# Down matrices of the experts loaded as one 16 KB run per partition, with a step of four in the gate/up products

## The chip, the cores and the metric

One core of a Trainium2 chip runs the whole program. The metric is the time of one execution on the device in microseconds, as the median of several runs. The profile comes from one further execution, taken by the hardware profiler.

## What is computed

A trunk of two layers over 512 tokens of 1024 channels, all in float32. Layer 0 mixes the tokens by latent attention with 16 heads, layer 1 by a bidirectional gated linear recurrence. Behind each mixer stands a mixture of 32 experts, of which each token uses two of one group of four:

```
idx, wts = route(ht, w_router, router_bias)        # two experts for each token
g, u = split(xb @ w_gu[e], 2)                      # w_gu[e]: 1024 x 1024, 512 gate and 512 up columns
y = (silu(g) * u) @ w_dn[e]                        # w_dn[e]: 512 x 1024
x = x + g2 * sum over the two experts of wts * y
```

Each expert has 4 MB of gate/up weights and 2 MB of down weights, and every expert of both layers is read once: 64 x 6 MB, about 400 MB.

## The kernel before

Before the experts of a layer run, its mixer, the norm, the router and a ranking of the tokens have run (the stages of `STAGES`). The change touches none of it.

**Blocks.** The expert work is cut into 60 blocks of 32 token rows per layer (`NB`, `ROWS`). A table `CAP` gives the busier experts up to five blocks and the quieter ones a single block; `RUN` and `BLOCKS` fix in which order they come, experts with many blocks mixed with those that have one. Which expert stands at which place is known at run time only: SP reads it from `order_i`. A loop over `more_i` could run blocks beyond the 60, for tokens that fit in none.

**Gathers and scatters.** GpSimd gathers 32 token rows for each block from `xn_dram` (L639), four blocks to a tile, and scatters each block's result to `ys_dram` (L646).

**TensorE.** A tile of four blocks is transposed by `rows_transposed` (L1030), whose stationary operand is read with a step of 8 floats (`chunk(1, k)`). `gate_up` (L1034 to L1041) runs for each block k = 0 to 7 over the 1024 channels, and for each k four products side by side, `s_` = 0 to 3: stationary is the block's transposed rows, 128 x 32, moving are 256 columns of the gate/up matrix (128 gate and the 128 up columns that belong to them), and the results go to partitions 32 s_ to 32 s_ + 31 of a PSUM bank. So four column tiles of 32 work beside each other, and quarter s_ of the hidden units lies in 32 partitions of its own. In float32 each product is two matmul records. A half of `gate_up` (four values of k) is 16 products, 32 records. Between the halves stands the transpose of the block before (L1044), behind them its down products.

ScalarE takes the silu of the gate part (L1362), VectorE multiplies with the up part (L1937), TensorE transposes the 128 x 128 result (L1044), ScalarE copies it (L1350). `down` (L1046 to L1051) then takes f = 0 to 3: stationary is piece f of the copy, 128 hidden units x 32 rows, moving are 256 of the 1024 columns of row group f of the down matrix. As quarter s_ of the hidden units is columns 128 s_ to 128 s_ + 127, row group f must hold rows 128 f to 128 f + 127 of the down matrix, one to a partition: this is what `dn_rows` (L423) says. VectorE scales the result by the token's weight and the gate (L1919).

**Weights.** A ring of three slots, each for one gate/up and one down matrix (`GU`, `DN`), is filled by SP alone, one matrix behind the other on its queue: `load_expert` (L506 to L514) waits until the gate/up products of the expert three places before are done (L510), issues the gate/up matrix (L511), waits for the down products of that expert (L513) and issues the down matrix (L514). The gate/up matrix is taken as `(p k) n -> p (k n)`: partition p holds rows 8p to 8p + 7, one run of 32 KB. The down matrix is taken as `(k p) n -> p k n`: partition p holds rows p, 128 + p, 256 + p and 384 + p, four runs of 4 KB. The matrices of the first two places are issued earlier, while the mixer's last products and the router run (L481 to L487 and L498 to L504). TensorE waits for the matrices at L1077 and L1062, when the first block of an expert comes.

Of the kernel before, what the change touches and what calls it, by code (L numbers as in the profile page):

```python
# [12 lines left out]
P = 128  # L13
# [18 lines left out]
FT = FE // P  # L32
# [16 lines left out]
TILES = P // ROWS  # L49
# [28 lines left out]
RING = 3  # L78
# [67 lines left out]
def trunk(nc, x, c, positions, norm_mix, norm_ffn, w_ada, b_ada, mla_w_in, mla_q_a_norm, mla_kv_a_norm,  # L146
# [4 lines left out]
    with ctx:  # L151
# [70 lines left out]
        def view(t, off, *dims):  # L222
            n = 1
            for d in dims:
                n *= d
            v = t[:, off:off + n]
            if len(dims) == 2:
                v = v.rearrange("p (a b) -> p a b", a=dims[0])
            elif len(dims) == 3:
                v = v.rearrange("p (a b c) -> p a b c", a=dims[0], b=dims[1])  # L230
            assert len(dims) < 4
            return v

        hT = view(arena, 0, KT, SEQ)
        w_in = view(arena, 4096, KT, LAT)
# [95 lines left out]
        S = {}  # L331
# [70 lines left out]
        DN = [view(ring_dn0, 0, FT, D), view(ring_dn1, 0, FT, D), view(arena, 8192, FT, D)]  # L402
# [14 lines left out]
        def gone(place, l):  # L417
            return NB * l + LAST[ORDER[place]] + 1

        def gu_rows(l, e):  # L420
            return moe_w_gu[l, e].rearrange("(p k) n -> p (k n)", k=KT)

        def dn_rows(l, e):  # L423
            return moe_w_dn[l, e].rearrange("(k p) n -> p k n", p=P)


        @block.sync
        def _(sp):
# [26 lines left out]
            def load_xb(b):  # L455
                xcols = slice(D + b * 2 * P, D + (b + 1) * 2 * P)
                sp.dma_start(w_xb, rnn_w_in[0][:, xcols].rearrange("(k p) n -> p k n", p=P)).then_inc(S["wx_in"], 16)

            def load_gt(b):
                gcols = slice(b * 2 * P, (b + 1) * 2 * P)  # L460
                sp.dma_start(w_gt, rnn_w_in[0][:, gcols].rearrange("(k p) n -> p k n", p=P)).then_inc(S["wg_in"], 16)

            def load_rg(b):
                for m, w in enumerate((rnn_w_rf, rnn_w_if, rnn_w_rb, rnn_w_ib)):
                    sp.dma_start(w_rg[:, 2 * m:2 * m + 2, :], w[0, b].rearrange("(k p) n -> p k n", p=P)
                                 ).then_inc(S["wr_in"], 16)

            for l in range(2):
                if l == 0:
                    sp.wait_ge(S["sq_used"], 2 * TT)  # L470
                    sp.dma_start(w_o, mla_w_o[0].rearrange("(k p) n -> p k n", p=P)).then_inc(S["w_o_in"], 16)
                    sp.wait_ge(S["ada_used"], 12)
                    for r in range(2 * KT):
                        for j in range(3):
                            if r:
                                sp.wait_ge(S["stage_used"], 3 * (r - 1) + j + 1)
                            ch = 3 * (r // KT) + j
                            sp.dma_start(stage[:, j, :], w_ada_v[1][:, r % KT, ch * D:(ch + 1) * D]
                                         ).then_inc(S[f"stage_in{j}"], 16)
                    sp.wait_ge(S["unit"], STAGES["proj0"] + 8)  # L480
                    sp.dma_start(GU[0].rearrange("p k n -> p (k n)"), gu_rows(l, 0)).then_inc(S["gu_in0"], 16)  # L481
                    sp.dma_start(DN[0], dn_rows(l, 0)).then_inc(S["dn_in0"], 16)
                    sp.wait_ge(S["xn_ready"], 4 * 2)
                    sp.dma_start(xn_dram.rearrange("(i p) d -> p i d", p=P), xn_moe).then_inc(S["xn_saved"], 16)
                    sp.dma_start(DN[1], dn_rows(l, 1)).then_inc(S["dn_in1"], 16)
                    sp.wait_ge(S["unit"], STAGES["ada1g"] + 4)
                    sp.dma_start(GU[1].rearrange("p k n -> p (k n)"), gu_rows(l, 1)).then_inc(S["gu_in1"], 16)  # L487
                else:
                    sp.dma_start(w_o, rnn_w_o[0].rearrange("(k p) n -> p k n", p=P)).then_inc(S["w_o_in"], 16)
                    for b in range(1, NBLK):  # L490
                        sp.wait_ge(S["unit"], STAGES[f"xb{b - 1}"] + 2)
                        load_xb(b)
                        sp.wait_ge(S["unit"], STAGES[f"gate_r{b - 1}"] + 2)
                        load_gt(b)
                        sp.wait_ge(S["unit"], STAGES[f"rg{b - 1}"] + 8)
                        load_rg(b)
                    sp.wait_ge(S["y_ready"], NBLK)
                    sp.dma_start(GU[1].rearrange("p k n -> p (k n)"), gu_rows(l, 1)).then_inc(S["gu_in1"], 16)  # L498
                    sp.wait_ge(S["unit"], STAGES["proj1"] + 8)
                    sp.dma_start(GU[0].rearrange("p k n -> p (k n)"), gu_rows(l, 0)).then_inc(S["gu_in0"], 16)  # L500
                    sp.dma_start(DN[0], dn_rows(l, 0)).then_inc(S["dn_in0"], 16)
                    sp.wait_ge(S["xn_ready"], 4 * 4)
                    sp.dma_start(xn_dram.rearrange("(i p) d -> p i d", p=P), xn_moe).then_inc(S["xn_saved"], 16)
                    sp.dma_start(DN[1], dn_rows(l, 1)).then_inc(S["dn_in1"], 16)  # L504

                def load_expert(n):  # L506
                    o = ORDER[n]
                    e = sp.value_load(order_i[o:o + 1, 0:1], min_val=0, max_val=NE - 1)
                    if n >= RING:
                        sp.wait_ge(S["gu_done"], gone(n - RING, l))  # L510
                    sp.dma_start(GU[n % RING].rearrange("p k n -> p (k n)"), gu_rows(l, e)).then_inc(S[f"gu_in{n % RING}"], 16)  # L511
                    if n >= RING:
                        sp.wait_ge(S["dn_done"], gone(n - RING, l))  # L513
                    sp.dma_start(DN[n % RING], dn_rows(l, e)).then_inc(S[f"dn_in{n % RING}"], 16)  # L514

                sp.wait_ge(S["order_ready"], l + 1)
                sp.wait_ge(S["more_ready"], l + 1)
                for n in range(2, NE):
                    load_expert(n)
                if l == 0:  # L520
                    sp.wait_ge(S["gu_done"], gone(NE - RING, l))
                    sp.wait_ge(S["dn_done"], gone(NE - RING, l))
                    load_xb(0)
                    load_gt(0)
                    load_rg(0)

                o = OV[l]
                sp.wait_ge(S["more_ready"], l + 1)
                n_more = sp.value_load(more_i[0:1, 31:32], min_val=0, max_val=MAX_EXTRA)
                sp.wait_ge(S["gu_done"], NB * (l + 1))  # L530
                sp.wait_ge(S["dn_done"], NB * (l + 1))
                with sp.Fori(0, MAX_EXTRA) as u:
                    with sp.If(n_more > u):
                        e = sp.value_load(more_i[0:1, bass.ds(u, 1)], min_val=0, max_val=NE - 1)
                        sp.wait_ge(o["dn_done"], u + 1)
                        sp.dma_start(GU[0].rearrange("p k n -> p (k n)"), gu_rows(l, e)).then_inc(o["w_in"], 16)
                        sp.dma_start(DN[0], dn_rows(l, e)).then_inc(o["w_in"], 16)

                sp.wait_ge(S["ov_done"], l + 1)
                for i in range(TT):  # L540
                    sp.dma_start(y_pair[i // 2][:, i % 2, :], y_rows[i]).then_inc(S[f"y_in{i}"], 16)
# [141 lines left out]
        def _(pe):  # L683
# [223 lines left out]
            for l in range(2):  # L907
# [126 lines left out]
                def gate_up(pb, rows, w, ks):  # L1034

                    for k in ks:
                        pair = w[:, k, :].rearrange("p (two s f) -> p two s f", two=2, s=TILES)
                        for s_ in range(TILES):
                            last = mm(ps[s_ * ROWS:(s_ + 1) * ROWS, pb, 0:2 * QF].rearrange("p (a b) -> p a b", a=2),  # L1039
                                      rows[:, k, :], pair[:, :, s_, :], start=(k == 0), stop=(k == KT - 1))  # L1040
                    return last  # L1041
# [27 lines left out]
                for n in range(NB):  # L1069
                    o, j = BLOCKS[n]  # L1070
# [22 lines left out]
                o = OV[l]  # L1093
# [19 lines left out]
        def _(act):  # L1113
# [167 lines left out]
            for l in range(2):  # L1281
# [33 lines left out]
                if l == 0:  # L1315
                    columns1("ada1a", 2)
                modulated(2 * l + 1)
                (_, g), = mine(f"logits{l}", 1, "A")
                act.wait_ge(S["unit"], g + 1)
                A(scores.rearrange("p i e -> p (i e)"), bank(g)[:, 0:TT * NE], ACT.Sigmoid).then_inc(S["a_free"], 1)  # L1320
# [669 lines left out]
```

## Time and profile before

| | |
|---|---|
| median of 3 runs | 1841.3 us (1840.11 to 1847.21) |
| profiled execution | 1844.75 us |
| its span | 1843.0 us |
| TensorE busy | 1459.4 us (79%) |
| DMA | 517.14 MB, mean 281 GB/s |
| expert stage of layer 0 | about 444 to 957 us |
| expert stage of layer 1 | about 1297 to 1808 us |

A busy time counts the moments in which at least one instruction of the engine runs. The DMA share is that of 16 engines, and a packet is one contiguous piece as an engine moved it. The clock granted to TensorE is at one of two levels, 1.2 or 2.4 GHz; the column PEclk is its mean as a part of the upper one.

### The profile page before, as it was taken

How to read it: one execution, taken by the hardware profiler on the slowest of the kernel's cores; microseconds unless marked ns; L12 is line 12 of the kernel's file. 1: busy time of each engine (PE TensorE's matmuls, PEld its weight loads, DVE VectorE, ACT ScalarE, POOL GpSimd, SP SyncE). 2: the span in 40 equal slices, each digit the busy share in tenths (PEclk: the TensorE clock that was granted, in tenths of full speed). 3: DMA queues.
4: the chain of work that ended last, by engine and by line, in shares of the span. 5: the costliest groups of instructions: out<-in, count | busy, mean ns of one | idle time of the engine just before them, and what ended most of it. 6: DMA issues, size and time to landing. Idle time of an engine off the chain costs nothing.

```text
span 1843.0 us, 34668 instructions
## 1 busy us (share of the span) xinstructions
PE 1459.4 (79%) x14391; PEld 834.5 (45%) x14391; DVE 656.7 (36%) x1130; ACT 340.1 (18%) x776; POOL 309.3 (17%) x356
## 2 busy tenths in 40 slices
PE   3999999997977877987744999796887678888852
PEld 3644777475533444544322444335454334444420
DVE  5674776745110111111103399875211111111102
ACT  3344444111100100111002233211111001111100
POOL 1001111001321222222100111100331113122200
PEclk9999999976988988999876999895898889899976
DMA  9634222575899999999974221034799999999994
GB/s 370 246 140 160 80 70 90 174 294 198 340 398 410 391 402 406 387 402 403 421 299 183 65 92 48 1 131 189 268 383 396 400 406 390 395 395 408 416 417 161
DMA packets 89853, 517.14 MB, mean 281 GB/s; under 512 B 12859, under 2 KB 25556, under 8 KB 80242
## 3 DMA queue, kind: packets, MB, share of 16 engines
q1 hardware_dynamic: 76176, 497.96, 69.1%
q0 software_dynamic: 11616, 16.85, 2.9%
q8 instruction: 110, 1.80, 0.4%
q10 hardware_dynamic: 1922, 0.29, 0.1%
q14 instruction: 29, 0.24, 0.0%
HBM read 507.70 MB, written 22.02 MB: 287 GB/s over the span
## 4 chain that ended last, share of the span: by engine, by line
PE 49%; DMA 33%; DVE 11%; issue 3%; ACT 2%; SPq 1%; POOLq 1%; POOL 0%; DVEq 0%; ACTq 0%
DMA ring_gu<-in_moe_w_gu_dram 26%; PE ps L1039 15%; PE ps L1049 7%; DMA arena<-in_moe_w_gu_dram 4%; PE ps L956 3%; PE ps L732 3%; PE ps L841 3%; PE ps L868 3%; PE ps L921 2%; DMA ring_gu<-in_w_ada_dram 2%; DVE ring_dn L1735 2%; PE ps L775 2%; PE ps L854 2%; PE ps L755 2%; PE ps L803 1%
## 5 line engine op out<-in xcount | busy, mean ns | idle before, releaser
L1039 PE MATMUL ps<-ring_gu,arena 128*32 128x256 f32 x4992 | 336.2, 409 | 120.8 <-DMA ring_gu<-in_moe_w_gu_dram 116.6
L1937 DVE TENSOR_TENSOR arena<-arena,ps 128x128 f32<-128x128 f32 x120 | 34.5, 288 | 748.0 <-ACT arena L1362 748.0
L1039 PEld LDWEIGHTS ps<-ring_gu,arena 128*32 128x32 f32 x4992 | 167.5, 116 | 246.5 <-DMA ring_gu<-in_moe_w_gu_dram 86.2
L646 POOL DMA_INDIRECT ys_dram<-arena,out_idx x120 | 118.9, 991 | 773.4 <-DVE arena L1919 757.0
L1039 PE MATMUL ps<-arena 128*32 128x256 f32 x2688 | 186.2, 419 | 76.3 <-DMA arena<-in_moe_w_gu_dram 75.2
L1049 PE MATMUL ps<-ring_dn,arena 128*32 128x256 f32 x2496 | 167.9, 382 | 18.0 <-issue 15.9
L1039 PEld LDWEIGHTS ps<-arena 128*32 128x32 f32 x2688 | 91.2, 119 | 148.0 <-issue 56.7
L1350 ACT ACTIVATE arena<-ps 128x128 f32<-128x128 f32 x120 | 33.3, 278 | 644.0 <-PE ps L1044 631.8
L639 POOL DMA_INDIRECT arena<-xn_dram,tok_idx x120 | 111.4, 928 | 92.8 <-DVE out_idx L1887 56.8
L1049 PEld LDWEIGHTS ps<-ring_dn,arena 128*32 128x32 f32 x2496 | 83.8, 110 | 86.3 <-issue 35.0
L921 PE MATMUL ps<-arena 128*128 128x512 f32 x256 | 110.6, 592 | 0.9 <-ACT arena L1163 0.9
L1919 DVE SCALAR_TENSOR_TENSOR arena<-ps,wtab,gate_bc 128x256 f32<-128x256 f32 x120 | 58.1, 484 | 139.4 <-PE ps L1049 133.2
L1049 PE MATMUL ps<-arena 128*32 128x256 f32 x1344 | 90.0, 380 | 9.2 <-issue 8.4
L1362 ACT ACTIVATE arena<-ps 128x128 f32<-128x128 f32 x120 | 33.3, 278 | 257.3 <-PE ps L1039 149.1
L921 PEld LDWEIGHTS ps<-arena 128*128 128x128 f32 x256 | 48.6, 190 | 61.9 <-issue 60.7
L841 PE MATMUL ps<-ring_dn 96*128 96x512 f32 x128 | 71.1, 641 | 0.9 <-DVE ring_dn L1604 0.9
L956 PE MATMUL ps<-ring_gu,ring_dn 128*128 128x512 f32 x128 | 57.1, 609 | 12.3 <-ACT arena L1302 12.3
L1049 PEld LDWEIGHTS ps<-arena 128*32 128x32 f32 x1344 | 45.0, 110 | 46.2 <-issue 18.9
L868 PE MATMUL ps<-arena 128*128 (+1 forms) x512 | 64.3, 269 | 0.0
L868 PEld LDWEIGHTS ps<-arena 128*128 128x128 f32 x512 | 62.2, 192 | 0.1
L721 PE MATMUL ps<-ident,arena 128*128 128x128 f32 x128 | 27.8, 390 | 41.7 <-DVE arena L1460 40.8
L1250 ACT ACTIVATE arena<-ps,mla_small 128x512 f32<-128x512 f32 x64 | 44.0, 687 | 84.1 <-DVE mla_small L1621 51.9
(311 smaller groups left out, 1709.8 us busy)
## 6 DMA issues: line engine op xcount, KB each, us to landing
ring_gu<-in_moe_w_gu_dram SPq DMA_DIRECT2D x44, 4096.0 KB
ring_dn<-in_moe_w_dn_dram SPq DMA_DIRECT2D x44, 2048.0 KB
arena<-in_moe_w_gu_dram SPq DMA_DIRECT2D x20, 4096.0 KB
arena<-in_moe_w_dn_dram SPq DMA_DIRECT2D x20, 2048.0 KB
ring_gu<-in_w_ada_dram SPq DMA_DIRECT2D x12, 2048.0 KB, 20.3
ring_gu<-in_w_ada_dram SPq DMA_DIRECT2D x48, 512.0 KB, 3.6
arena<-in_rnn_w_in_dram SPq DMA_DIRECT2D x8, 1024.0 KB, 6.2
ring_dn<-ys_dram SPq DMA_DIRECT2D x8, 1024.0 KB, 8.0
```

The costliest lines, as they stand in the source:

```text
L639: g.indirect_dma_start(xg[part, t % 2, :], None, xn_dram, bass.IndirectOffsetOnAxis(ap=tok_idx[0:ROWS, col:col + 1], axis=0), bounds_check ...
L646: g.indirect_dma_start(ys_dram, bass.IndirectOffsetOnAxis(ap=out_idx[:, col:col + 1], axis=0), yo[:, n % 4, :], None, bounds_check=2 * TIL ...
L732: last = mm(bank(g), src[:, k, i * P:(i + 1) * P], w_o[:, k, hf * HALF:(hf + 1) * HALF], start=(k == 0), stop=(k == KT - 1))
L755: last = mm(bank(g)[:, 0:width], hT[:, k, i * P:(i + 1) * P], w_in[:, k, hf * HALF:hf * HALF + width], start=(k == 0), stop=(k == KT - 1))
L841: mm(ps[:, 2 + qt, :], qT[0:QK, hb, qt * P:(qt + 1) * P], kT[0:QK, hb, :], start=True, stop=True).then_inc(S["s_ready"], 1)
L868: last = mm(ps[:, 7, qv * VH:(qv + 1) * VH], probsT[:, (p - 3) % 2, kt, :], kv_tok[:, kt, at(hv), NOPE:NOPE + VH].rearrange("p o d -> p (o ...
L921: last = mm(bank(g), w[:, k, m * P:(m + 1) * P], hT[:, k, :], start=(k == 0), stop=(k == KT - 1))
L956: last = mm(bank(g), yT[:, k, i * P:(i + 1) * P], w_o[:, k, hf * HALF:(hf + 1) * HALF], start=(k == 0), stop=(k == KT - 1))
L1039: last = mm(ps[s_ * ROWS:(s_ + 1) * ROWS, pb, 0:2 * QF].rearrange("p (a b) -> p a b", a=2), rows[:, k, :], pair[:, :, s_, :], start=(k == ...
L1049: last = mm(ps[s_ * ROWS:(s_ + 1) * ROWS, pb, 0:QD], src[:, f * ROWS:(f + 1) * ROWS], w[:, f, s_ * QD:(s_ + 1) * QD], start=(f == 0), stop ...
L1250: A(probs[:, p % 2, :], ps[:, 2 + p % 4, :], ACT.Exp, bias=nmax[:, p % 4:p % 4 + 1], accum_out=rsum[:, p // 4, p % 4:p % 4 + 1]).then_inc( ...
L1919: v.scalar_tensor_tensor(out=yo[:, n % 4, :], in0=ps[:, 5 + n % 2, 0:QD], scalar=wtab[:, col:col + 1], in1=gate_bc[:, 1, l * QD:(l + 1) * ...
```

## The change

The down matrix is read as `(p k) n -> p (k n)`: partition p holds rows 4p to 4p + 3, which lie behind one another in DRAM, one run of 16 KB. Row group f of the slot is then rows f, 4 + f, 8 + f, ... So that the hidden units agree, quarter s_ of the gate/up columns becomes the columns s_, 4 + s_, 8 + s_, ...: the moving operand of `gate_up` reads with a step of four floats, in both its gate and its up part. Outputs keep their shape and place; they hold other hidden units. `down` is not changed. The first lines below are the new layout, the last the new columns; the six other issues of down matrices change in the same way as the one of `load_expert`.

```
         def dn_rows(l, e):
-            return moe_w_dn[l, e].rearrange("(k p) n -> p k n", p=P)
+            return moe_w_dn[l, e].rearrange("(p k) n -> p (k n)", k=FT)
...
-                    sp.dma_start(DN[n % RING], dn_rows(l, e)).then_inc(S[f"dn_in{n % RING}"], 16)
+                    sp.dma_start(DN[n % RING].rearrange("p k n -> p (k n)"), dn_rows(l, e)).then_inc(S[f"dn_in{n % RING}"], 16)
...
                 def gate_up(pb, rows, w, ks):
 
                     for k in ks:
-                        pair = w[:, k, :].rearrange("p (two s f) -> p two s f", two=2, s=TILES)
+                        pair = w[:, k, :].rearrange("p (two f s) -> p two s f", two=2, s=TILES)
                         for s_ in range(TILES):
                             last = mm(ps[s_ * ROWS:(s_ + 1) * ROWS, pb, 0:2 * QF].rearrange("p (a b) -> p a b", a=2),
                                       rows[:, k, :], pair[:, :, s_, :], start=(k == 0), stop=(k == KT - 1))
```

## Rows read from the trace of the kernel before

**Rows 1.** The page: busy time of the engines, DMA share in 40 slices.

```profile
PE 1459.4 (79%) x14391; PEld 834.5 (45%) x14391; DVE 656.7 (36%) x1130; ACT 340.1 (18%) x776; POOL 309.3 (17%) x356
...
DMA  9634222575899999999974221034799999999994
GB/s 370 246 140 160 80 70 90 174 294 198 340 398 410 391 402 406 387 402 403 421 299 183 65 92 48 1 131 189 268 383 396 400 406 390 395 395 408 416 417 161
```

**Rows 2.** The page: the chain that ended last, shares of the span by line.

```profile
DMA ring_gu<-in_moe_w_gu_dram 26%; PE ps L1039 15%; PE ps L1049 7%; DMA arena<-in_moe_w_gu_dram 4%; PE ps L956 3%; PE ps L732 3%; PE ps L841 3%; PE ps L868 3%; PE ps L921 2%; DMA ring_gu<-in_w_ada_dram 2%; DVE ring_dn L1735 2%; PE ps L775 2%; PE ps L854 2%; PE ps L755 2%; PE ps L803 1%
```

**Rows 3.** Windows: length, busy of PE, PEld, DVE, ACT, POOL, clock, DMA share, GB/s.

```profile
500.00:940.00 440.00, 339.74 (x5107) 185.78 (x5099) 55.09 (x152) 46.81 (x156) 91.15 (x96) 0.89 1.01 403
1360.00:1790.00 430.00, 329.10 (x4950) 179.76 (x4946) 53.88 (x148) 44.55 (x148) 90.22 (x94) 0.90 1.01 404
```

**Rows 4.** Waits of PE, 500 to 940 us: us in total, times, longest.

```profile
PE ps L1039 <- DMA ring_gu<-in_moe_w_gu_dram: 50.8, 9, 10.7
PE ps L1039 <- DMA arena<-in_moe_w_gu_dram: 37.7, 7, 11.3
```

**Rows 5.** Waits of PE, 1360 to 1790 us.

```profile
PE ps L1039 <- DMA ring_gu<-in_moe_w_gu_dram: 51.2, 10, 11.1
PE ps L1039 <- DMA arena<-in_moe_w_gu_dram: 37.5, 7, 11.2
```

**Rows 6.** Chain in order of time, 900 to 957 us: start, us, what.

```profile
866.19 35.82 DMA ring_gu<-in_moe_w_gu_dram
...
902.25 3.45 PE ps L1039 x32
```

**Rows 7.** Windows, instructions of L1039 alone: busy of PE, PEld, clock, DMA, GB/s.

```profile
500.00:940.00 440.00, 223.62 (x3296) 110.99 (x3288) 0.89 1.01 403
1360.00:1790.00 430.00, 215.99 (x3204) 107.04 (x3200) 0.90 1.01 404
440.00:500.00 60.00, 30.97 (x488) 16.52 (x492) 0.88 0.83 318
1297.00:1360.00 63.00, 38.88 (x564) 18.89 (x568) 0.92 0.88 327
```

**Rows 8.** DMA, 1370.5 to 1373.5 us: packets, MB, share of 16 engines.

```profile
q1 hardware_dynamic: 303, 1.24, 102.4%
```

**Rows 9.** DMA, 1412 to 1418 us.

```profile
q1 hardware_dynamic: 80, 2.62, 101.4%
```

**Rows 10.** DMA, 500 to 940 us: the weights' queue, issues of down matrices.

```profile
q1 hardware_dynamic: 18149, 169.21, 95.6%
...
ring_dn<-in_moe_w_dn_dram SPq DMA_DIRECT2D x18, 2048.0 KB
...
arena<-in_moe_w_dn_dram SPq DMA_DIRECT2D x9, 2048.0 KB
```

**Rows 11.** DMA, 1360 to 1790 us; its ring_dn row is that of rows 10.

```profile
q1 hardware_dynamic: 17567, 165.79, 95.5%
...
arena<-in_moe_w_dn_dram SPq DMA_DIRECT2D x8, 2048.0 KB
```

**Rows 12.** Chain in order of time, 475 to 486 us, at full clock.

```profile
475.28 1.73 PE ps L1049 x32
477.01 1.73 PE ps L1039 x32
...
479.00 1.86 PE ps L1039 x32
```

**Rows 13.** Weight loads of two lines: duration ns min/median/max, first and last start.

```profile
L1030 PEld LDWEIGHTS ps<-ident,arena x240: 185/191/231, 447.5 to 1741.5; 128*128 128x128 f32 x120
...
L890 PEld LDWEIGHTS ps<-ident,ring_dn x32: 137/140/143, 325.1 to 328.4; 128*128 128x128 f32 x32
```

**Rows 14.** Instructions of PE in order of time: start, us, what.

```profile
489.99 1.04 PE L1030 MATMUL ps<-ident,arena 128*128 128x128 f32 x8
...
325.10 3.71 PE L890 MATMUL ps<-ident,ring_dn 128*128 128x128 f32 x32 [0.59 <-DVE ring_dn L1637]
```

**Rows 15.** Waits of SP's queue over the span.

```profile
SPq L514 <- PE ps L1049: 497.2, 58, 12.6
```

More of the change, by code:

```diff
@@ L423, in dn_rows @@
         def dn_rows(l, e):
-            return moe_w_dn[l, e].rearrange("(k p) n -> p k n", p=P)
+            return moe_w_dn[l, e].rearrange("(p k) n -> p (k n)", k=FT)
         @block.sync
@@ L481, in _ @@
                     sp.dma_start(GU[0].rearrange("p k n -> p (k n)"), gu_rows(l, 0)).then_inc(S["gu_in0"], 16)
-                    sp.dma_start(DN[0], dn_rows(l, 0)).then_inc(S["dn_in0"], 16)
+                    sp.dma_start(DN[0].rearrange("p k n -> p (k n)"), dn_rows(l, 0)).then_inc(S["dn_in0"], 16)
                     sp.wait_ge(S["xn_ready"], 4 * 2)
                     sp.dma_start(xn_dram.rearrange("(i p) d -> p i d", p=P), xn_moe).then_inc(S["xn_saved"], 16)
-                    sp.dma_start(DN[1], dn_rows(l, 1)).then_inc(S["dn_in1"], 16)
+                    sp.dma_start(DN[1].rearrange("p k n -> p (k n)"), dn_rows(l, 1)).then_inc(S["dn_in1"], 16)
                     sp.wait_ge(S["unit"], STAGES["ada1g"] + 4)
@@ L500, in _ @@
                     sp.dma_start(GU[0].rearrange("p k n -> p (k n)"), gu_rows(l, 0)).then_inc(S["gu_in0"], 16)
-                    sp.dma_start(DN[0], dn_rows(l, 0)).then_inc(S["dn_in0"], 16)
+                    sp.dma_start(DN[0].rearrange("p k n -> p (k n)"), dn_rows(l, 0)).then_inc(S["dn_in0"], 16)
                     sp.wait_ge(S["xn_ready"], 4 * 4)
                     sp.dma_start(xn_dram.rearrange("(i p) d -> p i d", p=P), xn_moe).then_inc(S["xn_saved"], 16)
-                    sp.dma_start(DN[1], dn_rows(l, 1)).then_inc(S["dn_in1"], 16)
+                    sp.dma_start(DN[1].rearrange("p k n -> p (k n)"), dn_rows(l, 1)).then_inc(S["dn_in1"], 16)
                 def load_expert(n):
@@ L513, in load_expert @@
                         sp.wait_ge(S["dn_done"], gone(n - RING, l))
-                    sp.dma_start(DN[n % RING], dn_rows(l, e)).then_inc(S[f"dn_in{n % RING}"], 16)
+                    sp.dma_start(DN[n % RING].rearrange("p k n -> p (k n)"), dn_rows(l, e)).then_inc(S[f"dn_in{n % RING}"], 16)
                 sp.wait_ge(S["order_ready"], l + 1)
@@ L536, in _ @@
                         sp.dma_start(GU[0].rearrange("p k n -> p (k n)"), gu_rows(l, e)).then_inc(o["w_in"], 16)
-                        sp.dma_start(DN[0], dn_rows(l, e)).then_inc(o["w_in"], 16)
+                        sp.dma_start(DN[0].rearrange("p k n -> p (k n)"), dn_rows(l, e)).then_inc(o["w_in"], 16)
                 sp.wait_ge(S["ov_done"], l + 1)
@@ L1036, in gate_up @@
                     for k in ks:
-                        pair = w[:, k, :].rearrange("p (two s f) -> p two s f", two=2, s=TILES)
+                        pair = w[:, k, :].rearrange("p (two f s) -> p two s f", two=2, s=TILES)
                         for s_ in range(TILES):
```

## Prediction

> **What bounds the kernel now.** I read the page first: how busy the engines and the DMA are by slice of the span, then the lines of the chain that ended last [rows 1, 2]. Two long stretches, the expert stages of the two layers, have the DMA at 9 tenths in nearly every slice and about 400 GB/s; the transfer of gate/up matrices alone is 26% of the chain, the products of L1039 and L1049 together 22%. Next I cut out the inner part of both expert stages by windows [rows 3]: 440 and 430 us, the DMA engines full (share 1.01), TensorE busy 340 and 329 us. The wait list of TensorE for the same stretches says for what it stands idle there [rows 4, 5]: 50.8 + 37.7 = 88.5 us and 51.2 + 37.5 = 88.7 us for gate/up matrices, and nothing for down matrices or gathered rows. The chain in order of time shows one such round [rows 6]: 36 us of DMA, some 10 us of products, again DMA. So in 870 of the 1843 us the stage ends when the weights have come through 16 full DMA engines, and TensorE has 177 us of slack. The first 60 us of each expert stage are otherwise: three slots are already loaded or loading, many blocks belong to the first experts, TensorE sets the pace, and a faster transfer is worth nothing there [rows 7].
>
> **Removed: small packets of the down matrix.** A down matrix of 2 MB moves now as four 4 KB runs per partition, 512 packets. A stretch in which only down packets moved has 303 packets in 102.4% of 16 engines' 3 us [rows 8]: 1.024 x 48 / 303 = 162.2 ns for 4 KB. One with gate/up packets alone has 80 in 101.4% of 16 engines' 6 us [rows 9]: 1217 ns for 32 KB, that is 152.1 ns for each 4 KB. These packets also show that a long run per partition is not cut up. The new size, 16 KB, isn't in the trace for weights. A straight line through the two gives 36.8 ns per KB (1054.8 / 28.67 KB) and 11.5 ns for each packet. 16.384 KB is then 614 ns, against 4 x 162.2 = 649: 34.6 ns less. Each engine moves 8 such pieces of a matrix: 0.28 us per matrix. The inner stretches issue 27 and 26 down matrices [rows 10, 11], so 53 x 0.28 = 14.7 us. Since the DMA is full and TensorE waits for what comes behind the down matrix in the same queue, each of these us comes off the end.
>
> The bound above: with gathers and scatters beside them packets are slower than that. In the first stretch [rows 10] 18149 packets with 169.21 MB are n of 4.096 KB and m of 32.768 KB: m = 3309, n = 14840. At the undisturbed prices they need 2407 + 4027 = 6434 us of engine time; the row has 95.6% of 16 x 440 = 6730 us. The 296 us over are 16.3 ns for each packet. If every packet that goes takes its 16.3 ns along, a matrix saves (34.6 + 3 x 16.3) x 8 = 0.67 us, together 35 us. If those 296 us belong to the gathers' own packets, which stay, it is 14.7. The bound below is 0: all of the 11.5 ns are drawn from two short stretches, and the price of a packet could lie in the run of 4 KB in the destination and not in the count. I take 17 us, near the lower of the two worked-out values, because the number of gather packets that must be let in between doesn't fall.
>
> **Added: moving columns with a step.** Each product of L1039 now streams 256 columns that lie 4 floats (16 bytes) apart, where before they were neighbours; counts, output and stationary operand stay. Now, at full clock, half of a block's gate/up work, 32 matmul records, takes 1.73 us [rows 12]: 8 rounds of four 32-column tiles side by side, 216 ns for 256 columns, 0.84 ns a column. No matmul before has a stepped moving operand, so the nearest is a stepped stationary one: the transposes of the gathered rows (L1030) load weights 8 floats apart. Their load takes 191 ns, that of the neighbouring columns at L890 140 ns [rows 13], 51 ns more for 128 columns. Yet 8 such transposes take 1.04 us, with 0.27 for the last to end 110 ns from one to the next; the 32 of L890 take 3.71, or 111 ns [rows 14]. So the step lengthens one load and leaves the pace alone, and that pace is 0.86 ns a column, the same as a gate/up stream needs. Ends for the unknown cost: 0 by the pace, and by the load's duration 51/128 = 0.4 ns on each of 256 columns, 102 ns on 216, +47% of gate/up work. It can't be a gain, since the stream already goes at the pace of the products with neighbouring columns in L1049. I take 0, the pace, because the gate/up work is a stream. What the row doesn't hold is four streams at once, each fetching anew for every column; that is rival one.
>
> What covers a small loss: the 177 us of waits. 3296 and 3204 records [rows 7] are 101.6 blocks at 3.6 us, 366 us of gate/up at full clock; a loss of p costs 366p there and hides up to p = 0.48. In the first 60 us of each stage nothing covers it: the last two lines [rows 7] have 30.97 + 38.88 = 70 us, so 70p is paid at once.
>
> A rule of the Trainium skill speaks against the change: SBUF — State Buffer, Specifications (TRN2), says that SBUF lines are 16 bytes and that full bandwidth needs at least two hits in a line, with a penalty for each crossing. Four floats are exactly one line, so each column would be its own line. By the rule the stepped loads of L1030 should already lose pace, and they don't; for four streams together no row decides. By the rule at its hardest the result is the second price of rival one, by the row it is the forecast.
>
> **The rest.** The order of hidden units changes, not a shape: the silu, the multiplication, the transpose of L1044 and the down products read and write what they did. SP issues the same number of DMAs and at L514 waits 497.2 us for the down products anyway [rows 15]. Gathers share the engines with longer packets, as they do now with 32 KB ones, and TensorE waits for none of them in the inner stretches [rows 4, 5]. Nothing for any of these.
>
> **Sum.** Profiled execution 1844.75 us (span 1843.0 and 1.75 around it), less 17: 1827.8. It lies 3.45 us above the median of the runs (1841.3); from the median the forecast is 1824 us.
>
> **Rival one: the stepped stream is slower.** For it: four tiles read at once, each with a fetch per column where one fetch now serves four. Against: a stepped load keeps 110 ns. Price: at p = 0.47 the inner stretches lose 172 us of work against 177 us of waits, so they come out about even with their DMA saving gone, with some 7 us more since the waits don't lie evenly; the starts pay 70 x 0.47 = 33: about 1881 us. At half pace (p = 1) 366 - 177 = 189, less some 45 us because a TensorE that never waits keeps its clock (a half block costs 3.45 to 3.64 us after a wait and 1.73 to 1.86 otherwise [rows 6, 12], and the 439.6 us of gate/up work [rows 7] are 74 over the 366 at full clock), and 70 at the starts: about 2055 us. It decides from p = 17/70 = 0.24: there the starts eat up the saving, and beyond it the kernel is slower.
>
> **Rival two: the saving doesn't arrive.** The engines may be held by what all packets pass, so that 16 KB moves like four times 4 KB, or gathers and scatters, waiting behind longer packets, give back what is won. For it: the stretches that gave the prices are 3 and 6 us long, and the share left over by gathers is larger than the saving (296 us of engine time against 14.7/2 x 16 = 118). Against: the rates, 4.096 KB in 162.2 ns against 4 x 8.192 KB in 1217, differ by 6.6%, and both stretches are full. It gives 1841 us, or 1834 if half arrives.
>
> **Chances.** Forecast 0.60, rival one 0.21, rival two 0.19. The forecast's own range is 1806 (35 us saved) to 1830. The range for 8 in 10 reaches through rival two and the start of rival one: 1806 to 1850; the body of rival one is outside. A measurement of this kernel can tell about 0.5%, 9.2 us, from no change. Faster than 1832: nearly all of the forecast and a fifth of rival two, 0.61. Within 9.2 us: the rest of the forecast, most of rival two and a rival one with p under 0.35, 0.19. Slower: 0.20.
>
> **What will show it.** No packets of 4 KB left from down matrices: 384 packets fewer for each, so 18149 become about 7800 in the same stretch, and about 430 GB/s where no gather runs. L1039 x32 still at 1.73 us in the chain; the load list of L1039 may show longer loads without a longer pace. Waits for gate/up shorter, stretch for stretch, by the 17 us. Wrong would be: L1039 x32 above 2.1 us (rival one), or the same duration of the inner stretches with fewer packets (rival two).

## The result: slower by 7.7%, and TensorE is now the bound of the expert stages

The changed kernel takes 1984.37 us (median of 5 runs, 1982.56 to 1989.41) against 1842.76 us for the kernel before in the same rounds. The ratio is 1.077, with an interval of 1.0753 to 1.0789. It lies far above the stated range of 1806 to 1850; of the cases of the prediction it is rival one that came.

The page of the changed kernel, as in [rows 1, 2]: busy time of the engines, DMA by slice, the chain's shares by line; then the largest group of instructions.

```profile
PE 1819.6 (92%) x14391; PEld 859.5 (43%) x14391; DVE 656.9 (33%) x1130; ACT 339.8 (17%) x776; POOL 308.8 (16%) x356
...
DMA  9534223757799978798874220073599989598884
...
PE ps L1039 44%; PE ps L1049 10%; PE ps L956 3%; PE ps L732 3%; PE ps L841 3%; PE ps L868 3%; PE ps L921 2%; DMA ring_gu<-in_w_ada_dram 2%; DVE ring_dn L1735 2%; PE ps L775 2%; PE ps L854 2%; PE ps L1044 2%; PE ps L1030 1%; PE ps L755 1%; PE ps L803 1%
...
L1039 PE MATMUL ps<-ring_gu,arena 128*32 128x256 f32 x4992 | 598.9, 632 | 3.7 <-ACT arena L1342 3.3
```

The gate/up transfer, 26% of the chain before, is gone from it, and L1039 has 44% where it had 15%. The idle time before this group of its products is 3.7 us in the whole span. The same windows as in [rows 3], and the weights' queue in the first of them, to be read against [rows 10]:

```profile
500.00:940.00 440.00, 440.00 (x4530) 176.40 (x4526) 49.07 (x135) 40.83 (x136) 88.67 (x93) 1.00 0.90 356
1360.00:1790.00 430.00, 422.81 (x4291) 169.20 (x4295) 51.81 (x143) 40.95 (x133) 89.89 (x94) 0.98 0.85 337
```

```profile
q1 hardware_dynamic: 6751, 148.87, 84.3%
```

TensorE is busy in all 440 us, at full clock, and its list of waits for this stretch is empty; the waits of [rows 4] have gone. The DMA share has fallen from 1.01 to 0.90: the transfer now waits for TensorE. The chain in order of time shows a whole block, which was 1.73 and 1.86 us for each half in [rows 12]:

```profile
601.97 1.73 PE ps L1049 x32
603.71 3.62 PE ps L1039 x32
607.32 0.26 PE ps L1044
607.58 3.74 PE ps L1039 x32
```

Each half of `gate_up` takes 3.62 to 3.74 us, the down products, whose columns still lie side by side, 1.73 us as before. From this the stage can be added up. A block is 1.73 + 3.62 + 0.26 + 3.74 = 9.35 us, 60 blocks 561, 14 transposes of tiles at 0.89 us 12.5: 574 us. The trace has 451.73 to 1028.9 in layer 0, 577 us. Before it was 507. The second stage is 579 us where it was 507. Together that is 142 us, and the spans differ by 1984.0 - 1843.0 = 141.

### The profile page after: what moved, and what is told of

The parts are those of the page before. It is cut to its first block, busy times and chain, and to the rows that moved or that the text cites. A ratio compares the mean times of both kernels' runs of the same rounds, so it can differ in the third digit from the quotient of the medians.

```text
span 1984.0 us, 34668 instructions
## 1 busy us (share of the span) xinstructions
PE 1819.6 (92%) x14391; PEld 859.5 (43%) x14391; DVE 656.9 (33%) x1130; ACT 339.8 (17%) x776; POOL 308.8 (16%) x356
## 4 chain that ended last, share of the span: by engine, by line
PE 81%; DVE 10%; DMA 4%; issue 2%; ACT 2%; POOLq 0%; SPq 0%; POOL 0%; DVEq 0%; ACTq 0%
PE ps L1039 44%; PE ps L1049 10%; PE ps L956 3%; PE ps L732 3%; PE ps L841 3%; PE ps L868 3%; PE ps L921 2%; DMA ring_gu<-in_w_ada_dram 2%; DVE ring_dn L1735 2%; PE ps L775 2%; PE ps L854 2%; PE ps L1044 2%; PE ps L1030 1%; PE ps L755 1%; PE ps L803 1%
## 5 line engine op out<-in xcount | busy, mean ns | idle before, releaser
L1039 PE MATMUL ps<-ring_gu,arena 128*32 128x256 f32 x4992 | 598.9, 632 | 3.7 <-ACT arena L1342 3.3
L1039 PE MATMUL ps<-arena 128*32 128x256 f32 x2688 | 321.8, 632 | 0.0
L1039 PEld LDWEIGHTS ps<-ring_gu,arena 128*32 128x32 f32 x4992 | 180.8, 124 | 306.3 <-issue 281.7
L1039 PEld LDWEIGHTS ps<-arena 128*32 128x32 f32 x2688 | 96.0, 124 | 162.1 <-issue 150.5
L1049 PE MATMUL ps<-ring_dn,arena 128*32 128x256 f32 x2496 | 151.4, 381 | 0.7 <-ACT arena L1350 0.7
L1350 ACT ACTIVATE arena<-ps 128x128 f32<-128x128 f32 x120 | 33.2, 277 | 627.9 <-PE ps L1044 622.5
L1049 PEld LDWEIGHTS ps<-ring_dn,arena 128*32 128x32 f32 x2496 | 89.1, 114 | 83.3 <-issue 46.0
L1049 PE MATMUL ps<-arena 128*32 128x256 f32 x1344 | 81.5, 381 | 0.0
L1049 PEld LDWEIGHTS ps<-arena 128*32 128x32 f32 x1344 | 49.4, 114 | 43.7 <-issue 25.2
L1044 PEld LDWEIGHTS ps<-ident,arena 128*128 128x128 f32 x120 | 16.6, 138 | 106.3 <-issue 106.3
```

The source lines that it names most:

```text
L1044: return tr(ps[:, pb, 0:P], src, ident[:, :])
L1049: last = mm(ps[s_ * ROWS:(s_ + 1) * ROWS, pb, 0:QD], src[:, f * ROWS:(f + 1) * ROWS], w[:, f, s_ * QD:(s_ + 1) * QD], start=(f == 0), stop ...
```

## Experiments

**Which half of the change is it?** e1 keeps the layout and takes the step out; e2 keeps the step and takes the layout back.

```
e1 (against the changed kernel):
-  pair = w[:, k, :].rearrange("p (two f s) -> p two s f", two=2, s=TILES)
+  pair = w[:, k, :].rearrange("p (two s f) -> p two s f", two=2, s=TILES)
e2 (against the kernel before): the same line, the other way round
```

> Down matrices as one 16 KB run per partition, gate/up columns without a step; so hidden units and rows of the down matrix are paired wrongly and only the times count. It isolates the transfer. If the saving of the forecast is real (0.28 us per matrix, about 53 matrices, 17 us taken), the median is about 1826 us and the chain shows 32 records of L1039 in 1.73 us as before. If the saving doesn't arrive (rival two), it is 1841 us.

> Step of four in the gate/up products, down matrices still as four 4 KB runs (pairing wrong, only times count). If the whole loss is the stepped stream, the time is that of the changed kernel, 1984 us, or a few us more, because TensorE and not the transfer is the bound in the expert stages. If the longer packets had a share in the loss, it comes out clearly lower, below 1970 us.

e1: 1832.58 us, ratio 0.9931 (0.9911 to 0.9951). e2: 1986.56 us, ratio 1.0773 (1.0752 to 1.0794). So the whole loss comes with the step; the packets have no share in it. The chain of e2 has the same halves:

```profile
478.82 3.62 PE ps L1039 x32
482.44 0.26 PE ps L1044
482.70 3.74 PE ps L1039 x32
486.44 1.73 PE ps L1049 x32
```

The weights' queue of e1, first for 500 to 940, then for 1360 to 1790 us:

```profile
q1 hardware_dynamic: 7879, 170.04, 95.1%
```

```profile
q1 hardware_dynamic: 7642, 166.32, 94.6%
```

Against [rows 10, 11] the packets fall from 18149 to 7879, and a MB takes 0.951 x 440 / 170.04 = 2.461 us of the 16 engines' time instead of 2.486, and 2.446 instead of 2.477: 1.0 and 1.3% less. What the queue moved in the same two windows rose less, by 0.5 and 0.3% (169.21 to 170.04 MB and 165.79 to 166.32).

**Is a smaller step free?** e3 takes two runs of 8 KB per partition and a step of 2 floats. It pairs hidden units and rows rightly.

```
-  return moe_w_dn[l, e].rearrange("(p k) n -> p (k n)", k=FT)
+  return moe_w_dn[l, e].rearrange("(a p b) n -> p a (b n)", a=2, b=2)
...
-  pair = w[:, k, :].rearrange("p (two f s) -> p two s f", two=2, s=TILES)
+  pair = w[:, k, :].rearrange("p (two a f b) -> p two a b f", two=2, a=2, b=2)
```

> A valid layout between the two: two runs of 8 KB per partition, and the moving columns 2 floats (8 bytes) apart. Theory A (what counts is how many 16-byte pieces a stream touches per column: a step of two touches one for two columns): four streams at 2.26 fetches per ns, the value of 4 x 256 columns in 453 ns, need 2 x 256 / 2.26 = 226 ns, so a half of gate/up takes 1.8 us, and the time is 1831 to 1838 us by a saving of 23 ns x 8 x 53 = 10 us. Theory B (any step costs the same): a half takes 3.6 us and the time is 1980 us.

1840.78 us, ratio 0.9987 (0.9974 to 1.0000). In its chain 31 of the 32 records take 1.82 us:

```profile
475.27 1.82 PE ps L1039 x31
```

Theory A is right to the number: a column costs half as much as with a step of four, and that is 227 ns for 256 columns, just above the 216 of the pace without a step. The time lies 2.8 us above the window that was given for it, and the saving is not clear of nothing. In its profile TensorE waits 13.2 us for the first gathered rows of layer 1, where the kernel before has 5.2; that wait comes up again with e6.

**Does a stream slow down alone, or do four streams share a limit?** e4 changes only the order of the products of the changed kernel.

```
+  side = 2 if l == 0 else 1
+  for s0, k in [(s0, k) for s0 in range(0, TILES, side) for k in ks]:
...
+      for s_ in range(s0, s0 + side):
```

> The changed kernel with its products in another order: in layer 0 only two 32-column tiles run side by side, in layer 1 one at a time, all with the step of four; the work is the same. Theory 1 (each stepped stream is slow by itself, 1.77 ns a column): a round of two and a round of one take 453 ns each, a half of gate/up 7.2 us in layer 0 and 14.5 us in layer 1, in all about 3600 us. Theory 2 (the streams share a limit of about 2.26 columns per ns): a round of two takes 226 ns, a half 3.6 us as with four streams, a round of one 216 ns and a half 6.9 us in layer 1; in all about 2340 us.

2744.7 us (one run): the time is neither 3600 nor 2340. In layer 1 a block with one tile at a time takes 19.3 us, and less the down products and the transpose that is 17.3 us for 64 records, 271 ns a record, between the 451 of theory 1 and the 216 of theory 2. The order in the program doesn't fix how many tiles run at once: records of the next tile start while those of the last are still running. So the time of e4 tells nothing apart. The starts of its records do: in the block of layer 1 from 1709 us they start singly or two together, and the next follow about 450 ns later either way (450 to 452 ns where single ones follow one another). In layer 0, from 508 us, two to four start together at the same beat. Theory 2 had 216 ns for one and 226 for two. The probes of e5 show it more plainly: each is a long series with one kind of stream. The code is abridged:

```
+  cols = flat[:, j * apart:j * apart + 256 * step].rearrange("p (f s) -> p f s", s=step)[:, :, 0]
...
+  for out_, rows_, cols_ in probe(tiles, apart, step):    # one source line for each kind
+      mm(out_, rows_, cols_, start=True, stop=True)
```

> The kernel before, with a row of probes behind the last product of layer 1 on TensorE: each a series of 24 products of 256 float32 columns (two records each) out of a weight slot, results unused, one source line per series. Full array with steps of 1, 2, 3, 4 and 8 floats; then 1, 2, 3 tiles of 32 columns with steps 1 and 4; 4 tiles with steps 1, 2, 3, 4, 8; 4 tiles with a step of 4 and starts 1024, 4 and 0 floats apart instead of 1. Theory 1 (a stepped stream is slow by itself, 1.77 ns a column): full array at step 4 takes 24 x 906 ns = 21.7 us against 10.2 at step 1, tiles at step 4 take 21.7, 10.9, 7.2 and 5.4 us for 1, 2, 3 and 4. Theory 2 (all streams share a limit, 2.26 columns per ns at step 4, and a stream's own limit is 1.2): full array 10.2 us at every step, tiles at step 4 take 10.2, 5.4, 5.4 and 5.4 us, at step 1 10.2, 5.1, 3.4 and 2.6; 4 tiles at step 2 take 2.7, at step 3 (three of four columns in a new 16-byte piece) 4.1, at step 8 5.4 us. If it is streams in the same 16-byte piece that hinder each other, starts 1024 floats apart give 2.6 us; if the limit is one of fetches in all, they stay at 5.4.

The chain of e5 in order of time, at full clock from L1124 on. L1124 to L1132: full array, steps 1, 2, 3, 4, 8. L1134 and L1136: one tile, steps 1 and 4. L1140, L1144, L1152: 2, 3, 4 tiles, step 4. L1156, L1158, L1160: 4 tiles with step 4, starts 1024, 4 and 0 floats apart.

```profile
1836.88 10.36 PE ps L1124 x48
1847.24 10.88 PE ps L1126 x48
1858.12 16.32 PE ps L1128 x48
1874.44 21.65 PE ps L1130 x48
1896.10 22.08 PE ps L1132 x48
1918.18 10.48 PE ps L1134 x48
1928.65 21.02 PE ps L1136 x47
...
1955.32 10.92 PE ps L1140 x48
...
1969.67 7.30 PE ps L1144 x46
...
1986.29 5.82 PE ps L1152 x47
...
1997.67 5.48 PE ps L1156 x48
2003.15 5.45 PE ps L1158 x48
2008.60 5.54 PE ps L1160 x44
```

Divided by 48 records, one stream alone takes 216, 227, 340, 451 and 460 ns for 256 columns. Theory 1 had 21.7 us for the full array at step 4; it is 21.65. Two, three and four tiles take 458 to 460 ns each side by side, counted from start to start, which halves, thirds and quarters the series. Theory 2 falls. The fetches don't hinder each other either: with columns that begin 1, 1024, 4 and 0 floats apart the series of four tiles takes 5.39, 5.44, 5.41 and 5.51 us from its first start to its last. One number fits all steps: with t = 1.77 ns for each 16-byte piece that a stream enters, 256 columns with a step of 2 enter 128 (227 ns), with a step of 3 192 (340), with 4 256 (453), with 8 the same 256 (measured 460), and with a step of 1 64 (113), less than the 216 ns that such a record takes anyway.

**Why did the row of L1030 promise otherwise?** It is a stationary operand, and it is a transpose. e9 takes both apart.

```
+  rows = flat[:, i * 128:i * 128 + P * step].rearrange("p (f s) -> p f s", s=step)[:, :, 0]
...
+  mm(out_, rows_, cols_, start=True, stop=True)     # 64 or 256 moving columns
...
+  tr(out_, rows_, ident[:, :])
```

> The kernel before with probes behind the last product of layer 1, 24 products each (48 records): stationary operand of 128 columns with a step of 1, 2, 4 and 8 floats and only 64 moving columns; then steps 1 and 8 with 256 moving columns; then 24 transposes with steps 1, 4 and 8. If a stationary operand is fetched under the limit that e5 showed for a moving one (1.77 ns for each 16-byte piece), a record with a step of 4 or 8 takes at least 128 x 1.77 = 227 ns with 64 moving columns, and a transpose 227 ns. If not, records with 64 moving columns take the same at every step (about 110 ns, the pace of L1030's transposes), and transposes 110 ns.

The chain of e9. L1120 to L1126: steps 1, 2, 4, 8 with 64 moving columns, while the lower clock was granted. L1130: step 8 with 256 moving columns at the upper clock. L1132, L1134, L1136: transposes with steps 1, 4, 8, at the upper clock.

```profile
1833.92 10.24 PE ps L1120 x48
1844.16 10.24 PE ps L1122 x48
1854.40 11.18 PE ps L1124 x48
1865.58 11.44 PE ps L1126 x48
...
1889.55 11.52 PE ps L1130 x48
1901.06 2.62 PE ps L1132 x24
1903.68 2.88 PE ps L1134 x24
1906.56 2.46 PE ps L1136 x22
```

In a product a stepped stationary operand is slower too: 213, 213, 233 and 238 ns, where 128 x 1.77 is 227, and 240 ns at the upper clock with 256 moving columns, against 216 in e5. In a transpose it is not: 109, 120 and 112 ns. The lower clock hides most of the difference in the first four, since without a step a record takes 213 ns there and not the 110 that was expected. At the upper clock the trace of the kernel before has the pair: L699 sums columns by products with a stationary operand of 128 columns and one moving column, and its stationary operand has a step of 8 floats or none (`chunk(u, k)` for odd and even `u`). The first row is with the step, the second without, both at a granted clock of 1.00:

```profile
80.77 3.83 PE L699 MATMUL ps<-ones,gate_bc 128*128 128x1 f32 x16
...
384.81 3.63 PE L699 MATMUL ps<-ones,ring_gu 128*128 128x1 f32 x32
```

That is 239 ns a record with the step and 113 without. The row on which the prediction leaned was of the kind that is exempt, and a row of the kind that pays stood in the same trace.

**Can the layout be had without the step?** Column 4j + k of quarter s is hidden unit 4p + k with p = 32 s + j, so all that is wanted is a transpose of 32 x 32 blocks. e6 does it on VectorE and drops L1044 and L1350. Hidden units and rows are paired rightly.

```
+  v.transpose(hmidT[:, n % 2, :], hmid[:, n % 2, :].rearrange("p (j k) -> p k j", k=FT))
```

> A valid kernel with the 16 KB runs and without a step on TensorE. Hidden unit 4p + k is column 4j + k of quarter s with p = 32 s + j, so the order that the down matrix wants is a transpose of 32 x 32 blocks of the 128 x 128 hidden tile, its columns read with a step of four; VectorE does it in one instruction, in place of the transpose of L1044 on TensorE and the copy of L1350 on ScalarE. Theory: the stage is bound by the transfer, so it shows the saving of the layout alone (1832.6 us, 0.993 of before) and takes besides 0.26 us of TensorE work for each of some 10 + 10 blocks at the start of the stages, where TensorE sets the pace: 5 us. 1826 to 1830 us. Against it: if VectorE's stepped transpose takes 1 us or more and delays the down products, 1833 us or above.

1836.49 us, ratio 0.9994 (0.9980 to 1.0007): no gain. In its profile the stages are shorter, but the wait of TensorE for the first gathered rows of layer 1 is 13.6 us, where the kernel before has 5.2:

```profile
PE ps L1030 <- DMA arena<-xn_dram,tok_idx: 13.6, 1, 13.6
```

SP had issued the third gate/up matrix sooner after the first gather (4.6 us, before 6.4, counted from where that gather's issue began), and the fourth gather landed 9.8 us after its issue where it took 2.7 before. e7 adds a wait to e6, e8 the same wait to the kernel before.

```
   sp.wait_ge(S["more_ready"], l + 1)
+  sp.wait_ge(S["gathered0"], ((NU + 1) // 2 * l + 1) * 16 * TILES)
```

> The valid kernel of e6 (16 KB runs, VectorE's block transpose, no step on TensorE) with one wait more: SP issues the third gate/up matrix of a layer only when the first tile's gathered rows have landed. In the profile of e6 that matrix was issued 4.6 us after the first gather of layer 1, before the fourth gather's rows had moved, and TensorE waited 8 us longer for them than in the kernel before, where SP happened to issue 6.4 us after. If that race is what ate the saving, e7 is 5 to 10 us faster than e6: 1827 to 1832 us where before is 1837 to 1843, ratio 0.994 to 0.997. If the saving was lost elsewhere (lower clock because TensorE does less), the ratio stays at 0.999.

> The kernel before with the same wait added and nothing else. In its profile SP lost no time to the gathers, so the wait should do nothing there: ratio 0.999 to 1.001. If the race is lost in a part of the executions before as well, up to 0.997.

e7: 1832.81 us, ratio 0.9976 (0.9958 to 0.9994), just above the 0.994 to 0.997 that was expected, and the wait is 5.4 us. e8: 1840.8 us, 1.0016 (0.9998 to 1.0035): no gain, and no loss clear of noise. Since they ran on other chips than e6, three kernels ran once more on one:

> The kernel of e6 once more, now on one chip with the two that follow, so that the three can be told apart. If the race between SP and the gathers costs what its profile shows (8 us in layer 1), it is 5 to 8 us slower than the next; if it was lost in that one profile only, they agree within 2 us.

> The kernel of e7 (block transpose on VectorE, third gate/up matrix behind the first gathers) on the same chip. Ratio 0.9976 as before if that was its value; near 0.993 if the chip of e7 was an unlucky one.

> The kernel of e1 (16 KB runs alone, pairing of hidden units wrong) on the same chip. Ratio 0.993 if the saving of the longer packets is as measured in e1. If e11 lies above it by 4 us or more, VectorE's transpose doesn't bring what it takes from TensorE, and part of the saving is lost with it.

e10, the kernel of e6: ratio 1.0007 (0.9987 to 1.0028). e11, that of e7: 1830.33 us, ratio 0.9977 (0.9960 to 0.9993). e12, that of e1: 0.9986 (0.9971 to 1.0002). The same wait again, of e10 and of e11 (its lines are one further down):

```profile
PE ps L1030 <- DMA arena<-xn_dram,tok_idx: 13.3, 1, 13.3
```

```profile
PE ps L1031 <- DMA arena<-xn_dram,tok_idx: 5.3, 1, 5.3
```

So the race is lost in both profiles of this kernel, and with the guard in neither; the medians differ by 7 us, though the intervals still overlap a little. It is not e6's alone: TensorE waits 13.2 us for the first rows of layer 1 in e3, and 9.5, 8.1 and 9.4 us for those of layer 0 in e1, e12 and e5, whose code up to the probes is the kernel before, so e1 and e12 have 3 to 4 us of such a wait in their profiles too. In all these stages SP had issued the matrix 3.9 to 4.4 us after the start of the first gather, and 5.5 us or more after it where TensorE waits 5.2 to 5.4 us. How often the race is lost in executions without a profile is not shown. e11 repeats e7: with all its work done rightly it is 0.23% faster than the kernel before, by intervals that end below 1. The saving of the layout alone did not repeat: 0.7% in e1, 0.14% in e12, with intervals that don't meet. Its size stays open between nothing and 16 us. The engines' time for a MB is 1.2 and 1.1% less in e12 (2.456 and 2.449 us), so that part repeats.

The packets of the traces show where half of it goes. In the inner stretches of e1 a 16 KB packet takes 614 ns in the median, the price worked out in the prediction, and 656 ns in the mean, where four of 4 KB took 4 x 174 = 696 before. But the 32 KB packets of the gate/up matrices beside them became longer, 1276 ns in the mean against 1258. Over 53 matrices the first is worth 40 x 8 x 53 = 17 us, and the second takes back 18 ns x 6818 / 16 = 8 us. The traces of e5, e8 and e9, with the old packets, have means of 1245 to 1257 ns for 32 KB, and those of e6, e7, e10, e11 and e12 have 1270 to 1282. Why they become longer is not shown.

## Why the prediction was wrong, by its steps

**What bounds the kernel** was right: before the change the transfer had the inner stretches, and in e1, with the products as they were, TensorE still waits for it.

**Small packets removed**: right in kind, too large in size. 14.7 us was worked out and 17 taken; the rate in e1 gives 1.0 to 1.3% of the inner stretches, some 10 us, and the two measured ratios 12.7 and 2.6 us. The price of the new packet was right (614 ns); what the sum left at nothing is that the gate/up packets beside it take 18 ns more. The upper bound, by which the removed packets take their share of the disturbance along, would be 4% of the inner stretches and is refuted: the disturbance stayed with the packets that are left.

**Moving columns with a step** is the step that failed. "I take 0, the pace, because the gate/up work is a stream" rested on the transposes of L1030 [rows 13, 14]. The term that was put at 0 is 3.62 to 3.74 us for a half of `gate_up` instead of 1.73 to 1.86. e9 shows that a transpose keeps its pace with a step of 4 or 8 while a product doesn't. The row was near in shape and far in kind; L699, a product, would have shown 239 against 113 ns. The upper end, 47% from the longer load of the same row, was no bound either: e5 has 451 against 216 ns, 109%.

**Rival one** named the right effect with the wrong mechanism. Four tiles at once had no part in it; each stream pays by itself. The 16-byte lines and the two hits of the Trainium skill, SBUF — State Buffer, Specifications (TRN2), describe what e5 measured, and the trace agrees: with two columns to a line 256 columns take 227 ns against 216, with one column to a line 451. I had weighed the rule against a row that could not test it.

**Its price** for half pace, 2055 us, was too high. I counted as slack the 177 us of waits in the inner stretches and a guess for the clock. The full count is by block: at full clock 1.73 + 0.26 + 1.86 + 1.73 = 5.6 us, 60 of them and the tile transposes 347 us, against 507 us of stage: 160 us of slack in each stage, not 88. The loss is 2 x 60 x (3.62 + 3.74 - 1.73 - 1.86) = 452 us, less 320: 132 us, where 142 were measured.

**Rival two**, taken by itself, is half right: the packets did become cheaper, but what arrives at the end is 12.7 us in e1 and 2.6 in e12, and by e12 alone it could be nothing.

## What to carry to other kernels

Before an access pattern with a step is put on a busy engine to make a transfer tidier, take the price of that very kind of instruction, operand and step from a probe; a transpose says nothing about a product. If a permutation is needed, put it where the elements are few: here on the 128 x 128 hidden tile and not on the weights, 64 times larger per block. The slack of an engine is the stage less its work at full clock, not the waits that a list shows; and a new order of issue can lose a race elsewhere, as that of SP and the gathers, which one wait decides.

## What the runs showed of the hardware

- A float32 moving operand of a product costs about 1.77 ns for each 16-byte piece that it enters, alone or with three others beside it, where that is more than the record takes anyway. The stream at steps 1, 2, 3, 4, 8: 216, 227, 340, 451, 460 ns for 256 columns (e5).
- A stationary one of 128 columns with a step of 8 makes a record of 239 ns, against 113 without a step (L699 before, at the upper clock), 1.87 ns a piece; e9 has 233 to 240 ns for steps 4 and 8.
- The limit is one in time and not in clocks: in the changed kernel 72 records of L1039 began at the lower clock, and a round of four side by side takes 454 ns there and 453 at the upper one; without a step a round takes 427 ns at the lower clock and 216 at the upper one.
- Float32 transposes of 128 x 128 are exempt: 109, 120, 112 ns for steps 1, 4, 8 of the stationary operand (e9).
- A VectorE transpose of 32 x 32 blocks over 128 x 128 float32, read with a step of four, takes 422 ns (120 of them in e7).
- A gather of 32 rows that is issued with a 4 MB matrix right behind it lands 9.8 us after its issue instead of 2.7 (e6, layer 1).
- With 16 KB in place of 4 KB packets beside them, 32 KB packets take 1276 instead of 1258 ns in the mean (e1).
